# Building the expert gates in two alternating buffers, with the one-hots scaled on ScalarE and rows moved to an earlier stage

## What is computed

```python
top_score, top_pos = lax.top_k(cand_score, PEER_TOPK)
expert_idx = jnp.take_along_axis(cand_idx, top_pos, axis=-1)
gate = jax.nn.softmax(top_score, axis=-1)
...
u_sel = jnp.take(expert_u, idx, axis=0)
act = gelu(jnp.einsum('tkd,td->tk', u_sel, hb)) * gb
v_sel = jnp.take(expert_v, idx, axis=0)
return jnp.einsum('tk,tkd->td', act, v_sel)
```

## Time and profile before

| | |
|---|---|
| median of the runs | 2982.95 us |
| profiled execution | 2975.43 us, span 2973.7 us |
| PE busy | 2803.9 us, 94% |
| VectorE (DVE) busy | 2233.4 us, 75% |
| ScalarE (ACT) busy | 1181.3 us, 40% |
| GpSimd (POOL) busy | 1533.8 us, 52% |
| mean granted clock of PE | 0.970 of full |
| DMA | 949.46 MB, mean 319 GB/s |

### The profile page before, as it was taken

How to read it: one execution, slowest core, us unless ns; L and a number is a source line. 1 busy time by engine, 2 the same in 40 slices (tenths; PEclk the granted TensorE clock), 3 DMA queues, 4 the chain that set the end, 5 groups by cost and what they waited for, 6 DMA issues and landing times.

```text
span 2973.7 us, 43212 instructions
## 1 busy us (share of the span) xinstructions
PE 2803.9 (94%) x17757; PEld 2643.4 (89%) x17757; DVE 2233.4 (75%) x3157; ACT 1181.3 (40%) x1387; POOL 1533.8 (52%) x664
## 2 busy tenths in 40 slices
PE   7899899988999989989999899999999999999998
PEld 6677788866879989989999899999999999999997
DVE  6756576766677789979997577777777777778786
ACT  6755532357323333333433333434333333333321
POOL 0000154222242367863334488888867777766662
PEclk9999999989999999999999899999999999999999
DMA  9737638863797868877789899999999999999995
GB/s 362 277 142 263 232 128 328 335 255 127 301 355 279 341 247 297 298 276 298 309 304 371 333 371 353 379 366 383 376 360 407 411 411 388 393 384 382 364 371 217
DMA packets 189485, 949.46 MB, mean 319 GB/s; under 512 B 18352, under 2 KB 77792, under 8 KB 79552
## 3 DMA queue, kind: packets, MB, share of 16 engines
q1 hardware_dynamic: 116704, 485.55, 43.5%
q0 software_dynamic: 60848, 440.59, 38.0%
q10 hardware_dynamic: 11808, 21.70, 1.9%
HBM read 906.46 MB, written 41.22 MB: 319 GB/s over the span
## 4 chain that ended last, share of the span: by engine, by line
PE 69%; DVE 11%; DMA 11%; ACT 5%; POOL 2%; issue 1%; SPq 1%; ACTq 0%; DVEq 0%
PE ps L1686 14%; PE ps L2034 8%; PE ps L2036 8%; PE ps L2035 8%; PE ps L1967 7%; PE ps L1965 6%; PE ps L1966 6%; PE ps L1950 4%; DVE ring_lo L1099 4%; PE ps L1673 4%; DMA ring_raw<-peer_v 3%; POOL ring_lo L617 2%; DVE ps L1341 2%; ACT ring_hi L689 2%; DVE hot_a L1535 2%
## 5 line engine op out<-in xcount | busy, mean ns | idle before, releaser
L617 POOL TENSOR_TENSOR ring_lo<-ring_raw,ring_hi 128x2048 fp32r<-128x2048 f32 x215 | 1000.1, 4652 | 701.5 <-ACT ring_hi L689 699.9
L689 ACT ACTIVATE ring_hi<-ring_raw 128x2048 fp32r<-128x2048 f32 x400 | 762.0, 1918 | 688.2 <-DMA ring_raw<-peer_u 222.8
L1965 PE MATMUL ps<-bT_hi,ring_hi 128*128 128x304 f32 x2048 | 629.3, 307 | 33.0 <-DVE ring_lo L1099 24.8
L2034 PE MATMUL ps<-a_hi,ring_hi 128*128 128x304 f32 x2048 | 629.3, 307 | 31.2 <-DVE ring_lo L1099 15.8
L2036 PE MATMUL ps<-a_hi,ring_lo 128*128 128x304 f32 x2048 | 624.7, 305 | 0.0
L1967 PE MATMUL ps<-bT_hi,ring_lo 128*128 128x304 f32 x2048 | 624.2, 305 | 0.0
L1966 PE MATMUL ps<-bT_lo,ring_hi 128*128 128x304 f32 x2048 | 623.3, 304 | 0.0
L2035 PE MATMUL ps<-a_lo,ring_hi 128*128 128x304 f32 x2048 | 621.8, 304 | 0.0
L1099 DVE TENSOR_TENSOR ring_lo<-ring_raw,ring_hi 128x2048 fp32r<-128x2048 f32 x185 | 452.6, 2462 | 174.9 <-ACT ring_hi L689 174.7
L1965 PEld LDWEIGHTS ps<-bT_hi,ring_hi 128*128 128x128 f32 x2048 | 392.5, 192 | 35.3 <-issue 30.2
L2034 PEld LDWEIGHTS ps<-a_hi,ring_hi 128*128 128x128 f32 x2048 | 390.8, 191 | 36.8 <-issue 27.2
(11 more groups left out here) (310 smaller groups left out, 3772.3 us busy)
## 6 DMA issues: line engine op xcount, KB each, us to landing
ring_raw<-peer_u SPq DMA_DIRECT2D x128, 1024.0 KB, 7.6
ring_raw<-peer_v SPq DMA_DIRECT2D x128, 1024.0 KB, 8.0
ring_raw<-w_in SPq DMA_DIRECT2D x80, 1024.0 KB, 5.4
ring_raw<-w_out SPq DMA_DIRECT2D x32, 1024.0 KB, 4.8
ring_raw<-w_query SPq DMA_DIRECT2D x32, 1024.0 KB, 6.5
g_pair<-gates_scratch SPq DMA_DIRECT2D x64, 320.0 KB, 8.8
gelu_scratch<-ahead ACTq DMA_DIRECT2D x72, 152.0 KB, 5.3
g_in<-gelu_scratch SPq DMA_DIRECT2D x72, 152.0 KB, 7.5
```

Of the source, the lines that this page charges most:

```text
L617: pool.tensor_tensor(ring_lo[s][:], ring_raw[s][:], ring_hi[s][:].bitcast(F32), ALU.subtract)\
L689: act.activation(ring_hi[place(n)][:], ring_raw[place(n)][:], ACT.Copy).then_inc(hi_ok[SLOT[n]], 1)
L1965: pe.matmul(dst, hi[:, e], bT_hi[:, k, 0:NEAR], start=(k == 0), stop=False)
L2034: pe.matmul(dst, hi[:, col], a_hi[:, par, e, :], start=(e == 0), stop=False)
```

## The change

1. A batch is 32 tokens (`GSTEP`), 8 groups, three pieces with 3, 3 and 2 groups; ten batches fill two buffers `gbuf[0]` and `gbuf[1]` in turn, and a batch's first copy waits for the stores of two batches before. A batch is stored in two DMAs of 1 MiB, one from SP and one from ScalarE at its third piece. Loads fetch the gates of four pieces at a time (`g_quad`).
2. `hot` is one `tensor_tensor` of 128 x 1024 elements that makes both kinds of one-hot, unweighted; ScalarE multiplies each of the four in place by the gate (`scales_upto`), up to two groups ahead of its copies. PE waits for the scaling. The ring of one-hots is 4 deep.
3. In positions 181 to 210 all low parts are made on VectorE (before: 20 there, 10 on GpSimd); in 211 to 215 GpSimd makes 4 (before 2). VectorE's loop puts its row between the comparisons.
4. Rows by stage, worked out from the two tables: 92 to 111 with attention 49, now 54; 112 to 127 26, now 29; 128 to 143 30, now 37 (three at every even position from 130); 144 to 180 27 both; 181 to 210 40, now 35; 211 to 215 5 both; down 75 both; last stretch 167, now 157. So 120 rows instead of 105 are done before position 144. The `out` row goes from position 287 to 279.
5. `acc_mid` shares row buffer 2, which the v3 rows therefore don't use; `a_hi`, `a_lo`, `g_in` move; some semaphores are shared by two uses.

```diff
-GSTEP = 64
+GSTEP = 32
+HOT_GROUPS = GSTEP // 4
-G_PARTS = 4
+G_PARTS = 2
@@ def lo_on_pool(n):
+    if AHEAD <= n < AHEAD + HOT_END:
+        return False
     if AHEAD <= n < DOWN:
-        return (n - AHEAD - HOT_FIRST) % len(HOT_BATCH) < 2
+        return (n - AHEAD - HOT_END) % 3 < 2
@@
-HOT_RING = 3
-HOT_BATCH = (4, 4, 4, 4, 0, 0)
-HOT_ROWS = (1, 1, 1, 1, 2, 2)
+HOT_RING = 4
+HOT_LEAD = 2
+HOT_BATCH = (3, 3, 2)
+HOT_ROWS = (1, 1, 1, 1, 1, 2)
-BATCH_END = [HOT_FIRST + len(HOT_BATCH) * _b + 3 for _b in range(BATCHES)]
+BATCH_END = [HOT_FIRST + len(HOT_BATCH) * _b + 2 for _b in range(BATCHES)]
@@ def fill_rows():
     for n in range(92, OUT_B):
-        ROWS_AT[n] = 1 if n % 4 == 2 else 2
+        ROWS_AT[n] = 2
     for n in range(OUT_B, AHEAD - 1):
-        ROWS_AT[n] = 0 if n == QUERY_B - 1 else 1 if n == QUERY_B - 2 or n % 4 == 3 and n < QUERY_B else 2
+        ROWS_AT[n] = 0 if n == QUERY_B - 1 else 1 if n == QUERY_B - 2 else 3 if n > QUERY_B and n % 2 == 0 else 2
@@ def row_buffers():
-        ... ([2] if ROW_POS[r] >= OUT_B else []) ...
+        ... ([MID_BUF] if ROW_POS[r] >= OUT_B and ROWS[r][0] != "v3" else []) ...
@@ SP
             for b in range(BATCHES):
                 load_upto(AHEAD + BATCH_END[b] + 4)
-                sp_eng.wait_ge(g_out, min(16 * (b + 1), N_HOT))
-                for g in range(G_PARTS // 2):
-                    sp_eng.dma_start(*gate_part(b, g)).then_inc(g_stored, 16)
+                sp_eng.wait_ge(g_out, min(HOT_GROUPS * (b + 1), N_HOT))
+                sp_eng.dma_start(*gate_part(b, 0)).then_inc(g_stored[b % 2], 16)
             def load_gates(q):
                 if q >= 2:
-                    sp_eng.wait_ge(act_made, 2 * q - 2)
+                    sp_eng.wait_ge(act_made, 4 * q - 4)
@@ ScalarE
-                if j == 0 and b:
-                    act.wait_ge(g_stored, 16 * G_PARTS * b)
+                if j == 0 and b >= 2:
+                    act.wait_ge(g_stored[b % 2], 16 * G_PARTS * (b // 2))
+            def scales_upto(count):
+                while scaled[0] < min(count, N_HOT):
+                    j = scaled[0]
+                    scaled[0] += 1
+                    act.wait_ge(hot_made, j + 1)
+                    for q in range(4):
+                        one = hots[j % HOT_RING][:, 0, q, :]
+                        last = act.activation(one, one, ACT.Copy, scale=selT[:, 2, 4 * j + q:4 * j + q + 1])
+                    last.then_inc(hot_scaled, 1)
                 for _ in range(HOT_AT[i]):
+                    scales_upto(jj + HOT_LEAD + 1)
                     copy_gates(jj)
@@ VectorE
-                for q in range(4):
-                    dve.tensor_scalar(hot_a[:, first + q, :], iota[:], selT[:, 0, tok + q:tok + q + 1],
-                                      selT[:, 2, tok + q:tok + q + 1], ALU.is_equal, ALU.mult)
-                dve.tensor_tensor(hot_b[:, first:first + 4, :], bcast(iota[:], [P, 4, NK], 1),
-                                  bcast(selT[:, 1, tok:tok + 4], [P, 4, NK], 2), ALU.is_equal).then_inc(hot_made, 1)
+                shape = [P, 2, 4, NK]
+                dve.tensor_tensor(hots[jj % HOT_RING][:], iota[:].unsqueeze(1).unsqueeze(1).broadcast_to(shape),
+                                  bcast(selT[:, 0:2, tok:tok + 4], shape, 3), ALU.is_equal).then_inc(hot_made, 1)
@@
-                    hots_upto(used + HOT_RING)
-                    rows_step(ROWS_AT[AHEAD + i])
+                    left = ROWS_AT[AHEAD + i]
+                    if not HOT_AT[i]:
+                        hots_upto(used + HOT_RING)
+                    for q in range(HOT_AT[i]):
+                        hots_upto(used - HOT_AT[i] + q + 1 + HOT_LEAD)
+                        if q == 1 and left:
+                            rows_step(1)
+                            left -= 1
+                    rows_step(left)
                     lo_upto(AHEAD + i + 2)
@@ PE
             def outers():
-                pe.wait_ge(hot_made, j + 1)
+                pe.wait_ge(hot_scaled, j + 1)
```

105 lines of the change are left out of this document (54 added, 51 removed).

## The result

The changed kernel takes 2995.47 us (median of 20 runs, 2974.93 to 3012.12); the kernel before, on the same chip, 2981.53 (2966.58 to 2997.83). The ratio is 1.0043, 95% interval 1.0027 to 1.006: slower by 14 us in the medians, where 35 less were forecast. Measured once more beside later experiments it was 1.0048 (1.0023 to 1.0074), 2997.07 us.

A forecast was written before the change was run, and what follows sets the result against it. PE, busy for 94% of the span, was taken as the bound, so only its waits or slow clock could give time. Terms: -25 - 8 + 0 + 2 + 8 + 1 + 5 - 18 = -35 us, from median 2982.95 to 2948; range 2918 to 2985.

The forecast's parts named there:

- the price of the rows taken to the projections: Positions 92 to 143: 15 more rows there (105 become 120) were put at +8, +1 and +5 us.
- Rows in 92 to 111, +8: Before attention: two more rows, at 106 and 110, on two buffers cost 10 us; +8 us, bounds +3 and +14.
- 112 to 127, +1 (0 to 6): Three buffers need 12.3 us for three rows, exactly what two rows a piece ask; +1 us, bounds 0 and +6.
- 128 to 143, +5 (0 to 16): Ten rows ask 40 us where PE takes 37.3; VectorE's two-piece lead absorbs most; +5 us, bounds 0 and +16.
- the third row at 142: At position 142 a third row is gathered after GpSimd's subtraction, and the last score squares wait for it; within +5 us.
- Hot, -25: Positions 181 to 210: VectorE falls below PE and batch-end waits go; -25 us, bounds -29 and -8.
- Between hot and down, -8: Pieces 67 to 71: half of the 14.5 us lost there comes back; -8 us, bounds -18 and +3.
- Down 0: Down stretch: gate loads half as many and twice as large cost nothing; 0 us, bounds -3 and +6.
- the `out` row +2: Store moved from position 287 to 279, where GpSimd makes every low part; +2 us, bounds 0 and +6.
- Last stretch, -18 (-28 to +5): Ten fewer rows: 21 of 23.2 lost us come back, 3 given for v3 rows; -18 us, bounds -28 and +5.
- the gathers starve the projections: Rival: gathers of about 12 us cost the projections some 66 us against gains of 49; 3000 us, chance 0.10.
- Its point of decision: For the rival of starved projections: a gather of about 12 us, making a round 14.5, 4.8 us a row with three buffers.

The follow-up runs named there:

- light gathers: The changed kernel with 28 of every 32 rows before position 144 fetching 16 of their 128 expert rows, all instructions kept: 2951.94 us, ratio 0.9892.
- The run with the order changed: The changed kernel with SP loading position 215 before it waits for the gates' stores and issues the first gate loads: 3001.88 us, ratio 1.0052.
- the edited old kernels: Kernel before with sum in row buffer 2 (2990.18 us); that plus four-piece gate loads (2994.33); with the change's last-stretch parts except the 32-token layout (2983.42).

## Why the prediction was wrong

The step that failed is the price of the rows taken to the projections: +14 in the sum, 39 and 46 us in the two profiles. With 14 there, the 2 and 21 us that the two profiled spans are longer would have been 23 and 10 shorter, so the forecast's sign fell on this step. Each of its three terms was too small, for a different reason.

- *Rows in 92 to 111, +8:* +14 and +15, at the edge of my bound and just beyond it. What I computed was right: two more rows on two buffers, 10 us. The landings there are 7.6 us (7.2 to 7.6 in all nineteen full profiles), the issue follows a freed buffer by 0.28, the round is 10.2, and from the last row of position 104 to the last before the norms 12 rows took 63.2 us and 14 take 71.7. What failed is that I moved five rows and priced two. The three at 94, 98 and 102, where three buffers are in turn, stood at nothing; the last row of position 104 now comes 5.6 us later (571.69 against 566.14). Gathers also land more slowly there: a median of 9.1 to 10.1 us in 470 to 560 in the nine profiles with the added rows, 8.3 to 9.6 in the ten without. The 9.5 of the window 530 to 604 above mixes this part with the faster one behind it.
- *112 to 127, +1 (0 to 6):* +9 and +14. "Three buffers need 12.3 us for three rows, and two rows a piece ask exactly that" named a stage with no slack and priced it at nothing. That is the step with the largest relative error. It is not that gathers land later there when more are asked: in 742 to 890 they take 9.0 us, and 9.8 before. The rows lengthen VectorE's list (three products, 6.6 us, and waits for rows of 9 to 15 us instead of 5 to 10), and what stands behind them, the sums `x1B`, then holds ScalarE: 30 to 35 us of waits in the twelve profiles with 29 rows, 20 to 24 in the seven with 26. I had no such chain in my sum. How the 11 us divide between bytes, buffers and VectorE's own time is open; with light gathers the stage took 150.9.
- *128 to 143, +5 (0 to 16):* +15.5. A gather every 4.2 us against 3.7 asked; I had computed 4.0 and then let VectorE's lead absorb the rest. That reading is borne out by the waits: VectorE's for high parts, which are its lead, fall from 27 to 9 us, and those for rows rise from 13.5 to 29.6. The lead is spent, and from there on PE pays. That the third row at 142 would hold the squares was a minor part: PE's wait for them is 7.9 us instead of 5.7.
- *Hot, -25:* -30, the mechanism right in each number that was forecast. VectorE 48.0 of 54 us, no batch-end wait, PE busy in all 54 us. Scalings are 390 ns long, and from the first of four to the copy behind them it is 1.17 us (1380.92 to 1382.09), 0.293 each from start to start: between my bounds, and just what I had estimated from the Trainium skill, "VectorE: DVE Perf Modes", section on the TRN2 errata. It changed nothing, as said.
- *Between hot and down, -8:* -2 to -3. The stall was handed to the next arrival, which my text allowed and then halved. The run with the order changed shows that the order of piece 215 does not set its length; that the group of transfers before the first down piece does is argued from where the waits went.
- *Down 0 and the `out` row +2:* the row's wait is 4.3 us against 5.5; the loads of four pieces' gates were not seen. Down as a whole had 477.9 and 486.0 us in two profiles of one kernel, so terms of this size can't be read from it.
- *Last stretch, -18 (-28 to +5):* -5 in one profile, +1 in the other. The direction is right (745 with 152 rows, 805 with 172), the size is open. I took one execution's stage, 766, as the base and asked nowhere which stages scatter. Against the 779 to 782 of the edited old kernels the change would gain 12 to 21 in four profiles of five (the fifth had 784), near the 18; but these are other kernels, so this excuses the forecast only if the 766 was a short execution.

In medians: rows alone cost 11 us (2986.93 to 2997.82), all else alone gained 9 (to 2977.65), together they lose 14. So 12 us are not additive, give or take some 10 (an estimate from the three intervals). No run explains them: if taking 15 rows out of the last stretch is worth more in the changed kernel (44 us against 21), the two parts together should come out faster than their medians added up, not slower. And with exactly the old rows, hot's 30 us reach the median as 20 only (2985.32 to 2965.29, 2984.46 to 2964.38). Where the other 10 go is not settled: the profiles that show the 30 lie 6 and 13 us below their own medians, and every stage that could hold them scatters by as much.

Of the rivals, the one given 0.10 happened in kind, "the gathers starve the projections". That its 3000 lies so near 2995 is luck: it had 66 us of loss in the projections against 49 of gain, and the two profiles have 39 and 46 against some 37 and 24 of gain. Its point of decision was wrong: a landing of 12 us was not needed, 7.6 to 10 did it. The rule of "DMA: Bandwidth & Descriptors" in the Trainium skill (about 358 GB/s from HBM) would have made the last stretch 843 us with 167 rows, where it took 766, and by the same estimate 813 with 157; the first profile of the changed kernel has 373 and 382 GB/s there over 200 us, and the stretch took 761 and 767, so it does not bind here either.

## What to carry to other kernels

Work that is moved to a stage "with room" must be priced by that stage's scarcest buffer, not by the engine's idle time: compute the round (issue, landing, use, release) over the number of buffers, do it for every part of the stage in which the number of buffers differs, and count every item that is moved. Where the round only just meets the demand, expect to pay the whole difference. Then ask what stands behind the new work in an in-order list: each late row here became a late low part or a late sum for another engine. And take a base from several executions: the last stretch differed here by 13 us between two profiles of one kernel.

## What the runs showed of the hardware

- A gather of 128 rows of 8 KB landed in a median of 7.2 to 7.6 us in 571 to 640 us, with 12 rows as with 14; in 8.3 to 9.6 or 9.1 to 10.1 in 470 to 560, without and with the added rows; in 9.0 to 10.0 in 742 to 890 whatever the rows. One of 16 rows takes 5.3.
- The low parts of VectorE and GpSimd are made one after the other, even where both engines have begun. A low part on VectorE takes 2.27 to 2.30 us; in the twenty profiles 127 of them are longer, 4.8 to 7.4 us, and each of these ends 2.14 to 2.16 us after a subtraction of GpSimd has ended. The one that begins first keeps its time: where VectorE's low part was first, it took 2.28 us and GpSimd's 4.6 to 6.7 instead of 4.5. Even the 128 x 16 product took 3.17 and 4.00 us, and ended 0.04 us after GpSimd's subtraction.
- The gather instruction on GpSimd is 0.94 us long when VectorE is idle (none of 90 in the changed kernel is longer than 1.01) and 1.7 to 3.1 us when VectorE makes a low part or multiplies a row with `h_far` beside it: 69 of the 73 long ones end 0.81 or 0.82 us after such an instruction.
- A 1 MiB store of GpSimd's queue was waited for 6.57, 7.27 and 11.30 us in three executions, and PE's wait behind it followed it (4.3, 5.5, 9.2).
